# Second mixture of experts: the four least-used ranked experts as two pairs instead of one group of four, nine units instead of eight

## The reference, cut to what matters

```
probs = jax.nn.softmax(logits, axis=-1)
pg = probs.reshape(-1, N_GROUPS, EXPERTS_PER_GROUP_2)
vals, idx = lax.top_k(pg, TOP_K)
g_sel = jnp.argmax(vals.sum(-1), axis=-1)
...
for e in range(N_EXPERTS_2):
    h = jax.nn.silu(t @ w_gate[e]) * (t @ w_up[e])
    y = y + gate_dense[:, e:e + 1].astype(t.dtype) * (h @ w_down[e])
```

## Time and profile before

| | us |
|---|---|
| median of 3 runs (lowest, highest) | 1610.24 (1609.32, 1611.37) |
| the profiled execution's own time | 1609.38 |
| its span in the trace | 1607.7 |
| PE busy | 1481.8 (92%) |
| DVE busy | 512.6 (32%) |
| ACT busy | 331.3 (21%) |
| second mixture, from PE's first up matmul to its last down matmul | about 1137.6 to 1583.0 |

### The profile page before, as it was taken

One profiled execution on the slowest core, in us unless ns is written; L12 is line 12 of the kernel. 1 busy time (PEld: TensorE's weight loads), 2 busy tenths in 40 slices (PEclk: granted clock), 3 DMA queues, 4 the chain that ended last, 5 costly groups with the idle time before them and its releaser, 6 DMA issues.

```text
span 1607.7 us, 21351 instructions
## 1 busy us (share of the span) xinstructions
PE 1481.8 (92%) x8241; PEld 968.6 (60%) x8241; DVE 512.6 (32%) x1089; ACT 331.3 (21%) x725; POOL 149.6 (9%) x170
## 2 busy tenths in 40 slices
PE   6899999999999999989999789999999999579996
PEld 2577776777678888875554449977443543134433
DVE  2567676676630311144221120052501111001002
ACT  2343344433331200021010011162100000000001
POOL 1333423234200000000000000000000000000000
PEclk9999999999999999999999999999999999799999
DMA  9711111111555445527999997405599999999993
GB/s 385 311 48 39 44 47 36 43 39 52 212 225 206 157 137 178 172 105 308 421 421 421 421 420 272 141 1 189 239 422 421 421 421 421 422 421 421 422 421 125
DMA packets 58573, 402.96 MB, mean 251 GB/s; under 512 B 6801, under 2 KB 6929, under 8 KB 12288
## 3 DMA queue, kind: packets, MB, share of 16 engines
q1 hardware_dynamic: 52704, 381.92, 59.0%
q0 software_dynamic: 5792, 19.95, 4.0%
HBM read 400.75 MB, written 1.10 MB: 250 GB/s over the span
## 4 chain that ended last, share of the span: by engine, by line
PE 73%; SPq 9%; DMA 6%; DVE 6%; issue 3%; ACT 2%; POOL 1%; DVEq 0%; ACTq 0%; POOLq 0%
PE bank L679 71%; SPq L506 9%; DMA ring<-in_moe 4%; DMA first_w<-in_moe 2%; DVE arena L1813 1%; ACT arena L1435 1%; POOL arena L621 1%; PE bank L1143 1%; DMA xc<-in_xc 1%; DMA decay_rows<-arena 0%; DVE arena L1895 0%; ACT hc L1435 0%; DVE arena L1863 0%; ACT L1445 0%; DVE arena L1867 0%
## 5 line engine op out<-in xcount | busy, mean ns | idle before, releaser
L679 PE MATMUL bank<-arena 128*128 128x128 f32 (+6 forms) x3088 | 491.6, 328 | 36.5 <-DVE arena L1865 15.6
L679 PEld LDWEIGHTS bank<-arena 128*128 128x128 f32 (+3 forms) x3088 | 385.6, 185 | 165.3 <-issue 74.5
L1435 ACT ACTIVATE arena<-bank 128x256 f32<-128x256 f32 (+2 forms) x374 | 161.9, 448 | 1084.5 <-PE bank L679 810.1
L679 PE MATMUL bank<-ring,arena 128*64 128x512 f32 (+2 forms) x1288 | 331.3, 633 | 37.1 <-DMA ring<-in_moe 21.9
L679 PEld LDWEIGHTS bank<-ring,arena 128*64 128x64 f32 (+2 forms) x1288 | 99.3, 136 | 206.1 <-issue 205.5
L679 PE MATMUL bank<-hc,head_w 128*128 128x512 f32 (+1 forms) x384 | 162.3, 525 | 7.0 <-DVE arena L1887 6.5
L2217 DVE TENSOR_TENSOR arena<-arena,bank 128x256 f32<-128x256 f32 x43 | 18.1, 421 | 339.9 <-ACT arena L1435 339.9
L679 PE MATMUL bank<-arena,ring 128*128 128x256 f32 x416 | 93.2, 380 | 1.5 <-DVE arena L1992 1.2
L679 PE MATMUL bank<-hc,ring 128*128 128x256 f32 x416 | 91.2, 379 | 0.0
L679 PEld LDWEIGHTS bank<-arena,ring 128*128 128x128 f32 x416 | 78.7, 190 | 13.9 <-DVE arena L1992 1.6
L679 PEld LDWEIGHTS bank<-hc,ring 128*128 128x128 f32 x416 | 78.4, 190 | 11.1 <-issue 0.8
(11 more groups left out here) (274 smaller groups left out, 1270.0 us busy)
## 6 DMA issues: line engine op xcount, KB each, us to landing
ring<-in_moe SPq DMA_DIRECT2D x161, 1024.0 KB, 23.3
ring<-in_dense SPq DMA_DIRECT2D x59, 1024.0 KB, 9.5
arena<-in_moe SPq DMA_DIRECT2D x40, 1024.0 KB, 24.4
hc<-in_moe SPq DMA_DIRECT2D x27, 1024.0 KB, 24.5
head_w<-in_moe SPq DMA_DIRECT2D x15, 1024.0 KB, 19.7
xc<-in_moe SPq DMA_DIRECT2D x15, 1024.0 KB, 26.8
o_heads<-in_moe SPq DMA_DIRECT2D x15, 1024.0 KB, 23.4
first_w<-in_moe SPq DMA_DIRECT2D x15, 1024.0 KB, 20.8
```

Of the source, the lines that this page charges most:

```text
L679: return nc.tensor.matmul(out, lhsT, rhs_, start=start, stop=stop, **kw)
L1435: return nc.scalar.activation(out, in_, func, **kw)
```

## The change

`NARROW[1]` goes from 10 to 14: there are only 14 ranked experts, so no quad is left, and ranks 10 to 13 become two pairs. The list of units grows from eight to nine, and `SECOND_ORDER` is written anew for nine entries.

```
-SECOND_ORDER = [0, 3, 1, 4, 7, 2, 5, 6]
+SECOND_ORDER = [0, 3, 1, 4, 5, 2, 6, 7, 8]
 FIRST_ORDER = [0, 1, 2, 6, 3, 7, 8, 4, 9, 10, 5]
 PLACE = [FIRST_ORDER, SECOND_ORDER]
 FIXED = (6, 2)
 CUT = (6, 2)
-NARROW = (6, 10)
+NARROW = (6, 14)
```

## The result

The changed kernel took 1613.02 us (median of 20 runs, 1609.91 to 1614.13), the kernel before 1610.26 us in as many (1607.21 to 1611.40). The ratio is 1.0018, with a 95% interval of 1.0011 to 1.0024: slower by 2.8 us, clear of zero. The ratio lies within the 0.2% that the prediction calls the same, but its interval reaches past it. The prediction said 1613.0; that it is met to 0.02 us is luck, since the interval alone leaves 1.8 to 3.9 us for the difference.

What follows compares the result with a forecast made beforehand. The prediction took the weight transfers to end the mixture, with PE waiting 36.3 us; after the change PE ends last, its steps putting the last down 2.8 us later. Added to the median 1610.24 this gives 1613.0 us, range 1610.3 to 1617.0.

Steps and rivals of the forecast that it cites:

- the same: Outcome within 0.2% (3.2 us) of the kernel before; chance 0.57.
- The transfers are the floor, and the floor does not move: Second mixture: 192 transfers of 1 MB before and after; the last lands just before 1579.40, as before.
- Nothing moves up to the fifth unit; then 50.45, 50.0, 50.3 and 50.3: PE's time per unit from first turn_h: u = 4 starts at 1347.7, 0.41 us saved before it; u = 8 at 1548.8.
- The last unit: PE's steps in u = 8: 14.28, 10.82 and 7.35 us, then 1.0 from last turn_h to last down, at 1582.2.
- The last down 2.8 us later: End of the mixture: last down at 1582.2 against 1579.40, the 28.3 us tail unchanged, so span 1610.5.
- No wait comes back: PE lags the landing of u = 4 to 8's last down weights by 21, 41, 32, 22 and 3 us, never waiting.
- The stream stays full: Places at u = 5's end leave 8.6 us from issue to landing, u = 2 left 10.0; no loss taken.
- The quad's further 11.2 us: Rest of the extra unit's 50.3 us after 36.3 of vanished waits, put to clock 0.85 and refilling in the quad.
- The stream still last: Rival: PE comes sooner, the last down again starts at 1579.4; 0 to + 1.8 us, chance 0.12.
- Starving: Rival: places free too late in u = 5 and u = 6, last landing slips; + 4 to + 12 us, chance 0.13.
- The whole unit: Rival: nothing hides the ninth unit, which costs 50.3 us, giving 1660; chance 0.02.
- Faster: Rival: more than 3.2 us gained, needing 6 us off PE's sum and a faster stream, or shorter tail; chance 0.05.

Runs made afterwards that it cites:

- experiment 1: Sums of units 1 to 3 of the second mixture cut to one of eight output blocks: changed kernel 1610.7 us (1.0003), kernel before 1609.6 us (0.9997).
- experiment 5: Changed kernel's nine units with both singles last, after seven pairs: 1646.1 us, ratio 1.0219 to the kernel before.
- experiment 4: Changed kernel's nine units with the two singles back to back, then five pairs: 1629.0 us, ratio 1.0116 to the kernel before.
- experiment 2: Kernel before with its eight units reordered so that the quad runs last: 1612.8 us, ratio 1.0018 to the kernel before.
- experiment 3: Kernel before with the quad run last, plus dummy matmuls in the last three waits of the mixture: 1610.4 us, ratio 1.0003 to the kernel before.
- ten units: Changed kernel with four singles instead of two, so ten units, singles and pairs in turn: 1663.9 us, ratio 1.0330 to the kernel before.

## Why the prediction was right

- *The transfers are the floor, and the floor does not move.* Shown by experiment 1: with PE's work cut, both kernels end 429.0 and 429.2 us after the first turn_h, released by the last transfer; before it was 429.3.
- *Nothing moves up to the fifth unit; then 50.45, 50.0, 50.3 and 50.3.* After taking off 1.51 us the first turn_h of u = 5 to 8 stands at 1398.20, 1448.20, 1498.50 and 1548.81, and I had 1398.2, 1448.2, 1498.5 and 1548.8.
- *The last unit.* I had 14.28, 10.82, 7.35 and 1.0; it took 14.28, 10.82, 7.38 and 0.91. The 0.33 us by which the old step was longer was refilling after waits, and leaving it out was right.
- *The last down 2.8 us later.* 2.80 in the trace, 3.0 against the measured floor of experiment 1, 2.8 in the medians (1.8 to 3.9 by the interval). The span was put at 1610.5 and came out at 1612.2: 1.5 us lay ahead of the mixture, 0.2 in the tail.
- *No wait comes back.* True, but the lags that I listed were wrong in size. I had 21, 41, 32, 22 and 3 us; with the issue order counted rightly (experiment 5) they are 16, 31, 22, 12 and 3, again by calculation and not measured. Only the last decides, and it had no such error, since nothing follows it.
- *The stream stays full.* True. The comparison with u = 2 carried it (a place, the one with the shortest time, took 10.9 us from issue to landing there, 11.1 here), not the sums of 8.6 and 10.0 us left, which rested on the same wrong lag. Experiment 4 shows an order in which it does not.
- *The quad's further 11.2 us are a lowered clock and refilling.* The trace of the kernel before bears this out in the main. In the quad, behind two of its waits:

```profile
1380.30 1.03 PE L679 MATMUL bank<-ring,arena 128*32 128x512 f32 x1 [5.26 <-DMA first_w<-in_moe]
...
1390.24 5.12 PE L679 MATMUL bank<-ring,arena 128*32 128x512 f32 x32 [4.96 <-DMA ring<-in_moe]
```

  A matmul takes 1.03 us there where 0.59 is usual, a part 5.12 where 3.64 is the earlier trace rows. Six parts behind waits are slowed so, each by 1.3 to 1.7 us; that makes some 9 of the 11.2 us (an estimate from these rows), and refilling is left with about 2.
- *The rivals.* The stream still last: excluded, the last down waits for ACT. Starving: it exists as a mechanism (experiment 4), but not in this order. The whole unit: wrong here, and right for the tenth. Faster: nothing of it was seen.

## What to carry to other kernels

Where a stream of weights and an engine race, keep a ledger of the lag, unit by unit: it tells which work is nearly free (the ninth unit, 2.8 of 50 us), where it stops being free (the tenth, all 50), and that the order counts at both ends, since lag beyond the buffers starves the stream and lag used up too early can't be saved for later. Count in the ledger in the order in which the transfers are issued, not in the order of use. And look at the clock of the last piece of work behind the last transfer: waits just ahead of it made that piece 2.6 us slower.

## What the runs showed of the hardware

- What a wait costs depends on what stands around it. Waits of 3.5 to 4.8 us between parts of 5 to 6 us went with a granted clock of 0.67 (experiment 2), 26 waits of up to 1.3 us with 1.00 (experiment 5). The length of the last wait alone does not tell: after one of 2.5 us the clock was down (experiment 4, 0.83 in the 10 us around it), after two of 3.1 and 3.3 us with dummies ahead of them it was up (experiment 3, 1.00).
- With 1 MB transfers the stream held 420 GB/s (nine units, 1420 to 1470 us) while one took 11 to 15 us from issue to landing, by place. It ran at 377 GB/s (ten units, 1400 to 1500 us), where PE holds it back, with a median of 8 to 9 us in five of the seven places:

```profile
ring<-in_moe SPq DMA_DIRECT2D x22, 1024.0 KB, 8.9
arena<-in_moe SPq DMA_DIRECT2D x5, 1024.0 KB, 8.3
```
